# Splitting the residual norms of a six-layer transformer kernel, and the linears on both sides of them, into two token halves

## The reference, cut to what matters

```
def rmsnorm(x, g):
    xf = x.astype(jnp.float32)
    y = xf * lax.rsqrt(jnp.mean(xf * xf, axis=-1, keepdims=True) + EPS)
    return (y * g.astype(jnp.float32)).astype(x.dtype)

def modulate(h, shift, scale):
    return h * (1.0 + scale[:, None, :]) + shift[:, None, :]

x = x + branch(rmsnorm(x, g))                      # first two layers
x = x + gate * branch(modulate(rmsnorm(x, g), shift, scale))   # last four
```

## Time and profile before

| | |
|---|---|
| median of 3 runs | 2716.55 us (2713.75 to 2718.53) |
| the profiled execution | 2716.53 us, its span 2714.7 us |
| PE busy | 2551.2 us, 94% of the span |
| DVE busy | 1097.1 us, 40% |
| ACT busy | 472.1 us, 17% |
| mean granted TensorE clock | 0.955 |
| one modulation tile on DVE (L1274, 192 of them) | 1.28 us |

### The profile page before, as it was taken

One profiled execution on the slowest core, in us unless ns is written; L12 is line 12 of the kernel. 1 busy time (PEld: TensorE's weight loads), 2 busy tenths in 40 slices (PEclk: granted clock), 3 DMA queues, 4 the chain that ended last, 5 costly groups with the idle time before them and its releaser, 6 DMA issues.

```text
span 2714.7 us, 30366 instructions
## 1 busy us (share of the span) xinstructions
PE 2551.2 (94%) x11412; PEld 2007.7 (74%) x11412; DVE 1097.1 (40%) x2258; ACT 472.1 (17%) x1119; POOL 109.7 (4%) x211
## 2 busy tenths in 40 slices
PE   7789999998798999999999889999999999999997
PEld 4365888645467888488888568888788886688886
DVE  3754112244733022242564345644755552332321
ACT  1122100014502000111210222102123101102210
POOL 0000000000000001000011001010000110000000
PEclk9769999995899999999999899999999999999998
DMA  6123467630034567334778227784327774433441
GB/s 228 57 78 131 152 193 235 209 140 3 1 134 161 165 224 248 131 133 140 255 252 298 102 86 253 254 291 168 119 94 257 254 275 168 170 124 133 151 152 54
DMA packets 122173, 452.81 MB, mean 167 GB/s; under 512 B 13760, under 2 KB 13888, under 8 KB 121408
## 3 DMA queue, kind: packets, MB, share of 16 engines
q1 hardware_dynamic: 92880, 338.24, 35.7%
q0 software_dynamic: 29168, 112.80, 12.3%
HBM read 449.93 MB, written 1.05 MB: 166 GB/s over the span
## 4 chain that ended last, share of the span: by engine, by line
PE 89%; DVE 6%; issue 3%; ACT 2%; DMA 0%; SPq 0%; DVEq 0%; ACTq 0%; POOL 0%
PE pair L450 85%; PE bank L450 3%; DVE att_s L1196 1%; DVE arena L1191 1%; ACT arena L876 1%; PE bank L550 0%; ACT arena L888 0%; DVE arena L1605 0%; DVE arena L1601 0%; ACT arena L867 0%; DMA cst<-consts_dram 0%; PE bank L577 0%; DVE arena L1449 0%; DVE arena L1206 0%; DVE h L1113 0%
## 5 line engine op out<-in xcount | busy, mean ns | idle before, releaser
L450 PE MATMUL pair<-h,ring 128*128 128x256 f32 x5120 | 1123.3, 383 | 24.6 <-issue 24.6
L450 PEld LDWEIGHTS pair<-h,ring 128*128 128x128 f32 x5120 | 982.6, 192 | 164.1 <-issue 28.2
L450 PE MATMUL pair<-arena,ring 128*128 128x256 f32 x3312 | 722.4, 380 | 3.7 <-issue 2.1
L450 PEld LDWEIGHTS pair<-arena,ring 128*128 128x128 f32 x3312 | 630.3, 191 | 93.4 <-issue 3.5
L450 PE MATMUL pair<-ring,h 128*128 128x512 f32 (+1 forms) x768 | 331.7, 593 | 19.7 <-issue 16.7
L450 PEld LDWEIGHTS pair<-ring,h 128*128 128x128 f32 x768 | 146.6, 195 | 200.3 <-issue 192.3
L1274 DVE CUSTOM_DVE_ANT_0 adat<-adat,crow,cols 128x1024 f32<-128x1024 f32 x192 | 242.0, 1277 | 4.2 <-DMA adat<-adaw_dram 4.1
L1252 DVE SCALAR_TENSOR_TENSOR arena<-pair,cols,arena 128x255 f32<-128x255 f32 x176 | 84.9, 482 | 294.2 <-ACT arena L924 294.2
L847 ACT ACTIVATE h<-x 128x256 f32<-128x256 f32 x120 | 49.3, 416 | 855.9 <-DVE x L1122 474.9
L924 ACT ACTIVATE arena<-pair,cols 128x256 f32<-128x256 f32 x176 | 99.4, 565 | 477.0 <-PE pair L450 477.0
L1122 DVE SCALAR_TENSOR_TENSOR x<-pair,fin,x 128x256 f32<-128x256 f32 x64 | 30.9, 483 | 345.7 <-PE pair L450 345.7
(11 more groups left out here) (191 smaller groups left out, 1165.3 us busy)
## 6 DMA issues: line engine op xcount, KB each, us to landing
ring<-stream_dram SPq DMA_DIRECT2D x638, 512.0 KB, 3.9
adat<-adaw_dram POOLq DMA_DIRECT2D x192, 512.0 KB, 4.6
arena<-gmrows_dram POOLq DMA_DIRECT2D x2, 2560.0 KB, 10.4
arena<-cmpw_dram POOLq DMA_DIRECT2D x1, 2112.0 KB, 7.9
x<-x_in_dram SPq DMA_DIRECT2D x2, 512.0 KB, 4.6
arena<-mem_in_dram SPq DMA_DIRECT2D x1, 1024.0 KB, 12.8
arena<-gmws_dram POOLq DMA_DIRECT2D x2, 512.0 KB, 12.4
out_dram<-h POOLq DMA_DIRECT2D x1, 1024.0 KB, 4.1
```

What stands on the lines that cost most here:

```text
L450: return nc.tensor.matmul(out, lhsT, rhs, start=start, stop=stop)
```

## The change

`TAIL = HEAD = 2` and `HALVES` (tokens 0 to 127, and 128 to 255) are new. In the linear in front of a norm, groups 6 and 7 are computed as four: both for half 0 into the usual banks, then both for half 1 into banks 2 and 3 (`LATE`). A kind F behind a norm (but not `memk`) computes its groups 0 and 1 the same way, in the usual banks. A matmul of a half streams 128 tokens in place of 256, and each weight tile of these groups is loaded twice. The norm's squares of groups 6 and 7, its sum, root, reciprocal, products and shifts are done per half. The sum of half 0 stands inside the group 6 of half 1, the sum of half 1 behind the second matmul of the group that follows (second group of a kind F, first of a kind T and of `memk`). `mix0` and the memory's own norm stay whole. The output goes out in two transfers.

```diff
+TAIL = HEAD = 2
+HALVES = (slice(0, P), slice(P, TOK))
...
+        LATE = (2, 3)
...
+            def linear(name, moving, ready=None, after=None, norm=None, head=0):
...
+                def half(n, first, i):
+                    if i == 0:
+                        bank_free(g + n)
+                    for k in range(lin.K):
+                        if ready is not None:
+                            ready(n, k, i)
+                        if tail and n == first and i == 1 and k == min(6, lin.K - 1):
+                            norm_sum(norm, 0)
+                        bank = banks[(g + n) % 2 if not tail or i == 0 else LATE[n - first]]
+                        last = mm(bank[:, HALVES[i]], tile(t + n * lin.K + k),
+                                  moving(k)[:, HALVES[i]], k == 0, k == lin.K - 1)
+                        release(last, i == 1 and k < lin.K - 1, t + n * lin.K + k)
+                    if i == 1:
+                        last.then_inc(sem("mm_done"), 1)
+                    elif tail:
+                        last.then_inc(sem("half_done"), 1)
...
+                    for i in range(TT):
+                        for n in range(head):
+                            half(n, 0, i)
+                    for n in range(head, lin.N - tail):
+                        whole(n)
...
+                    for i in range(TT):
+                        for n in range(lin.N - tail, lin.N):
+                            half(n, lin.N - tail, i)
...
+            def squares(name, shift=None):
...
+                for i in range(TT):
+                    for n in range(TAIL):
+                        k = DK - TAIL + n
+                        if i == 0:
+                            act.wait_ge(sem("x_half"), TAILS[name] + n + 1)
+                        else:
+                            act.wait_ge(sem("freed_dve"), FREER[lin.g0 + k][1])
+                        nc.scalar.activation(h[:, k, HALVES[i]], x[:, k, HALVES[i]], ACT.Square
+                                             ).then_inc(sem("sq_done"), 1)
+                    root(name, HALVES[i], i)
+                    for k in range(DK if shift is not None else 0):
...
             def residual(name, norm, gain, gate=None, between=None):
...
+                for i in range(TT):
+                    for n in range(DK - TAIL, DK):
+                        if i == 0:
+                            dve.wait_ge(sem("half_done"), TAILS[norm] + n - (DK - TAIL) + 1)
+                            add(n, HALVES[0]).then_inc(sem("x_half"), 1)
+                            if n == DK - TAIL:
+                                add_squares(n - 1, slice(0, TOK), n)
+                        else:
+                            dve.wait_ge(sem("mm_done"), lin.g0 + n + 1)
+                            add(n, HALVES[1]).then_inc(sem("freed_dve"), 1)
+                    add_squares(DK - TAIL, HALVES[i], DK - TAIL + TAIL * i + 1)
+                    normalise(norm, gain, i)
...
-                residual("down0", "mix1", None, ada_tiles((2, 2, 2, 2, 2, 2, 1, 0)))
+                residual("down0", "mix1", col("norm_mix1", 0, DK), None, ada_tiles((3, 2, 2, 2, 2, 2)))
...
-            pool.wait_ge(sem("out_ready"), 1)
-            pool.dma_start(out_d, h[:, :, :]).then_inc(sem("out_done"), 16)
-            pool.wait_ge(sem("out_done"), 16)
+            for i in range(TT):
+                pool.wait_ge(sem("out_ready"), i + 1)
+                pool.dma_start(out_d[:, :, HALVES[i]], h[:, :, HALVES[i]]).then_inc(sem("out_done"), 16)
+            pool.wait_ge(sem("out_done"), 16 * TT)
```

More of the change, by code:

```diff
@@ L461, in tile, with release @@
                 return ring[:, at:at + n * P]
[L463 to L467, removed]
+            def release(ins, free, t):
+                n = t // SLAB - released[0]
+                if n > 0 and free:
+                    ins.then_inc(sem("slab_used"), n)
+                    released[0] += n
             def bank_free(g):
@@ L650, in body @@
                 pe.wait_ge(sem("o_read"), U_DSA[1])
-                linear("ab_out", lambda k: oT[:, k, :], None, with_norm("mem0"))
+                linear("ab_out", lambda k: oT[:, k, :], norm="mem0")
                 memory(0, "ffn0")
                 ffn(0, "mix1")
-                linear("nsa_in", lambda k: h[:, k, :], h_ready("mix1"))
+                linear("nsa_in", lambda k: h[:, k, :], h_ready("mix1", "T"))
                 turns("nsa_q", "nsa_normed")
@@ L684, in body @@
                 pe.wait_ge(sem("o_read"), U_NSA[2][1])
-                linear("nsa_out", lambda k: oT[:, k, :], None, with_norm("mem1"))
+                linear("nsa_out", lambda k: oT[:, k, :], norm="mem1")
                 memory(1, "ffn1")
@@ L721, in body @@
                         pe.wait_ge(sem("o_read"), U_MLA[1])
-                        linear("mla_o", lambda k: oT[:, k, :], None, with_norm(f"ffn2_{i}"))
+                        linear("mla_o", lambda k: oT[:, k, :], norm=f"ffn2_{i}")
                     else:
-                        linear("hg_f", hin, h_ready(f"mix2_{i}"))
+                        linear("hg_f", hin, h_ready(f"mix2_{i}"), head=HEAD)
                         linear("hg_q", hin)
@@ L965, in body @@
                 attention(*U_DSA)
-                squares("mem0", x, h)
+                squares("mem0")
                 memory(0, "ffn0")
                 gates("up0", 0)
-                squares("mix1", x, h)
+                squares("mix1")
                 roots("nsa_sums", 1, stat[:, 1, 0:TT * 24], P, 1.0 / HD, "nsa_root")
@@ L989, in body @@
                     attention(*U_NSA[kind])
-                squares("mem1", x, h)
+                squares("mem1")
                 memory(1, "ffn1")
                 gates("up1", FT)
-                squares("mix2_0", x, h)
+                squares("mix2_0", mod[:, 0, 0:DK])
                 for i in range(LAYERS2):
-                    shifts(f"mix2_{i}", mod[:, i, 0:DK])
                     if i % 3 == 0:
@@ new lines, in add @@
+                def add(n, cols):
+                    late = cols == HALVES[1]
+                    b = banks[LATE[n - (DK - TAIL)] if late else (lin.g0 + n) % 2][:, cols]
+                    if gate is None:
+                        return V.tensor_tensor(x[:, n, cols], b, x[:, n, cols], ALU.add)
+                    return V.scalar_tensor_tensor(x[:, n, cols], b, gate[:, n:n + 1], x[:, n, cols], ALU.mult, ALU.add)
+                for n in range(DK - TAIL):
+                    dve.wait_ge(sem("mm_done"), lin.g0 + n + 1)
+                    add(n, slice(0, TOK)).then_inc(sem("freed_dve"), 1)
@@ L1639, in body @@
                         attention(*U_MLA)
-                        residual("mla_o", f"ffn2_{i}", gate)
+                        residual("mla_o", f"ffn2_{i}", gain, gate)
                     else:
```

246 lines of the change are left out of this document (126 added, 120 removed).

## The result

The changed kernel took 2688.2 us (median of 4 runs, 2682.85 to 2691.4), the kernel before 2717.5 beside it: a ratio of 0.9891, 95% interval 0.9879 to 0.9904. That is 29 us less where 42 were forecast. The profiled execution took 2688.3 us with a span of 2686.5. Two executions in the experiments, one of the kernel before (4656.4 us) and one of the kernel of experiment 1 (5368.0 us), ran far slower than all others and are left out of every ratio and median given here.

What follows compares the result with a forecast made beforehand. TensorE was taken to bound the kernel, through stalls and a lowered clock at the norms. From 2716.53 us: - 28.0 (stalls) + 8.5 (halves) - 19.5 (clock) - 3.2 (end) = - 42.2, that is 2674 us; range 2662 to 2692.

Steps and rivals of the forecast that it cites:

- What bounds the kernel, and the price of a norm before: TensorE is 89% of the chain; norms cost 55.7 us of its stall plus 23.9 us of lowered clock.
- Price of a half matmul: Tail and head groups: one matmul every 0.112 us, 520 tiles costing 8.1 us more, 8.5 with the sums.
- the rival of the weight loads: Half matmuls of tails and heads bound by weight loads of 0.19 us: up to 162 us more, 2836; chance 0.04.
- The dry ring: Rival: weight ring runs dry behind six tails, up to 3.9 us each, up to 2697; chance 0.05.
- Stall by kind of norm: Stalls left at each norm, by K and the next linear's kind: 27.7 us in place of 55.7, 28.0 saved.
- The clock: Behind eleven norms: stalls of 1.7 and 2.1 keep it up, 3.8 mostly not; 4.4 of 23.9 left, 19.5 us saved.
- The end: From PE's last matmul to the kernel's end: last product after 5.2 us in place of 8.0; 3.2 us saved in all.
- what else moves: Modulation tiles in `down` and later slab release in the ring: both hidden, no time added.
- more than 5 as a sign: Attention stages: a change of more than 5 us would show the prediction wrong.
- The rival that the clock still falls everywhere: At nine norms with stalls left the clock falls, about 2.1 us each, 14.5 given back: 2689; chance 0.18.

Runs made afterwards that it cites:

- experiment 1: Changed kernel, but the first two groups behind a split norm wait only until DVE has read half 0 of groups 6 and 7; 2669.8 us, ratio 0.9828.
- experiment 5: Kernel before, plus seven matmuls of no use behind the sum of each of eleven norms; 2692.7 us, ratio 0.9919.
- experiment 3: Changed kernel, but layer 2's modulation tiles of groups 0 to 4 are done in groups 6 to 17; 2681.1 us, ratio 0.9853.
- experiment 6: Unchanged reruns: kernel before 2720.2 and 2718.1 us; changed kernel 2678.2, 2677.6 and 2686.9; kernel of experiment 1 2676.8.
- experiment 2: Changed kernel, but with a stall put back at the four norms in front of a kind T; 2697.9 us, ratio 0.9927.

## Why the prediction was right, and where its size was off

- **What bounds the kernel, and the price of a norm before: right.** 55.7 us of stall and 23.9 of clock were read from the trace, and experiment 5 took 23.7 us away by the clock alone.
- **Price of a half matmul: right.** The changed kernel starts the matmuls of the tails from `ring` every 0.111 to 0.112 us (788 intervals in the bank of half 1), so 8.1 us for 520 tiles stands, and the rival of the weight loads falls. The dry ring falls too: the only transfer that PE waits for in the changed kernel is that of the constants at the start, 11.0 us as before.
- **Stall by kind of norm: right, to 0.3 us where the clock came out as forecast.** Kind T: forecast 4.4 + 2.6 - 0.7 = 6.3 less at `mix1`, measured 6.35. `ffn2_0`: 5.1 - 1.7 - 0.7 + 2.7 = 5.4 forecast, 5.1 measured. `mix2_2` with its extra wait for ACT: 2.9 and 2.9. `ffn2_1`: 5.1 - 3.8 - 0.5 + 1.6 = 2.4 and 2.1. `mem0`: 0.9 + 0.3 longer, measured 1.2 longer. The sum over all norm stretches was to be 42.2 less and was 40.4. Experiment 1 shows that at K = 4 and 8 the cause is the one named, the bank behind DVE's order.
- **The clock: right where the stall is gone, under-sized where one of 2 to 4 us is left.** I took it that a stall of 2.1 keeps the clock up. It did at `ffn2_1`, but at `ffn2_2` it fell in two of four traces of the changed kernel (0.76 in the window at 2022.93), at 1.5 us, with the same wait in all four:

```profile
2022.93 3.62 PE L460 MATMUL pair<-h,ring 128*128 128x128 f32 x20 [1.92 <-DVE x L1186]
```

Behind `ffn1` it fell in all four traces, as forecast, behind `ffn0` in three. In the profiled execution the three windows miss 0.39, 0.24 and 0.24 of 7 us, 6.1 us together, where I had left 4.4: the difference of 1.7 is about the 1.8 by which the norm stretches fell short.
- **The end: right.** From the last matmul to the last product 8.0 before and 5.2 after, with 0.2 less behind it: 3.0 for 3.2.
- **The step that failed is "what else moves", as hidden.** I looked at the slabs of the ring and at DVE's own tiles, but not POOL's queue at `gm_free`, which the change moves with the end of DVE's half 1. That costs 2.9 to 4.9 us in `cup2`; experiment 3 gets them back. The mechanism is a rival that I did not have: a transfer that starts relative to DVE while PE has moved ahead.
- **The rest of the miss is in the execution that was profiled.** 8.2 us lie in the two attention stages, which vary by 4 and 7 us from trace to trace. I had allowed 5 for both together and named more than 5 as a sign that the prediction is wrong. That sign came: the allowance was too small. The kernel before alone covers the first stage (199.7 to 202.4 in three traces); in the second an effect of the change is neither shown nor excluded (experiment 6). Taking 42.2 - 1.8 (norm stretches) - 4.4 (`cup2`) - 8.2 + 0.5 = 28.3 closes the account of the profiled pair (28.2) up to rounding. The range, 2662 to 2692, held it, near its upper end. Two of the three further executions of the changed kernel, at 2678, lie nearer to the forecast.
- **The rival that the clock still falls everywhere** (2689) has nearly the measured time and is wrong: the clock behind eight of the eleven norms is 1.00. The time alone would not have told the two apart; the windows do.

## What to carry to other kernels

Count at each wait of TensorE both the wait and the stretch behind it at the lower clock; here the second was 24 of 80 us, and filler matmuls (whose result nobody reads) alone took it away. When work is split so that one engine runs ahead, ask of each semaphore what data it really stands for (a bank's half 0, not the group's last addition), and where the other engines' orders put their signals relative to the one that now leads, transfers on other queues among them. When executions differ by more than an effect, cut the trace at events that both kernels have and compare stretches: most of them here repeat to 0.1 us, while the whole varies by 10.

## What the runs showed of the hardware that was not expected

- Stalls of 0.7 and 2.3 us with a sum between them brought the clock down to its lower level in all four places of experiment 2 (window clock 0.76). Stalls of 1.93 and 0.93 with 4 us of work between did not at `ffn2_1` in four traces of the changed kernel, while 1.92 did at `ffn2_2` in two of four: the same program, the same stall, and the clock falls in one execution and not in the other. Behind the 3.41 of `ffn0` it stayed up in one of four.
- Matmuls whose result nobody reads kept the clock at 1.00 behind all eleven norms with a stall of 3.4 to 3.9 us, at no cost that the stretches show.
- The time of one program varies by more than 10 us (2677.6 to 2688.3 in four traces of the changed kernel) while most stretches of dense matmuls repeat to 0.1. What varies are the two attention stages, the norms `ffn0` and `ffn2_2`, and the stretch from `cup2` to `cdown2` with its wait for a transfer.
